# First attention's grouped queries and keys computed channel-first, two heads of different groups in each pair

## The reference

```
proj = jnp.einsum('bsd,df->bsf', h, w_in)
c_q, c_kv, k_r, q_s, k_s, v_s = _split_cols(proj, AB_SPLITS)      # 384, 256, 32, 512, 128, 128
logits = jnp.einsum('bcqkgd,bcskd->bckgqs', qc, kb) * d ** -0.5 + alibi
p = jax.nn.softmax(jnp.concatenate([logits, sink], -1), axis=-1)[..., :-1]
o = jnp.concatenate([o_a.reshape(B, S, -1), o_b.reshape(B, S, -1)], -1)
return jnp.einsum('bsf,fd->bsd', o, w_out)
```

## Time and profile before

| | |
|---|---|
| time, three runs | 923.5 us median (923.07 to 923.65) |
| profiled execution | 923.53 us, span 921.4 us, granted clock 0.999 |
| PE, PEld | 907.3 us (98%), 760.9 us (83%) |
| DVE, ACT, POOL | 607.7 us (66%), 507.5 us (55%), 37.0 us (4%) |
| DMA | 72,556 packets, 169.39 MB, mean 184 GB/s |
| DMA packets under 512 B | 11,304 |

### The profile page before, as it was taken

One profiled execution on the slowest core, in us unless ns is written; L12 is line 12 of the kernel. 1 busy time (PEld: TensorE's weight loads), 2 busy tenths in 40 slices (PEclk: granted clock), 3 DMA queues, 4 the chain that ended last, 5 costly groups with the idle time before them and its releaser, 6 DMA issues.

```text
span 921.4 us, 12745 instructions
## 1 busy us (share of the span) xinstructions
PE 907.3 (98%) x4734; PEld 760.9 (83%) x4734; DVE 607.7 (66%) x999; ACT 507.5 (55%) x816; POOL 37.0 (4%) x53
## 2 busy tenths in 40 slices
PE   7999999999999999999999999999999999999997
PEld 5888878888888898877888888877888888888875
DVE  4888687766663767768766666376656577574665
ACT  4785564655552456666455555255457664655434
POOL 1100034000000001000000000001000000000000
PEclk9999999999999999999999999999999999999999
DMA  8754456755574578443855557354663465545651
GB/s 312 258 183 137 141 191 200 269 190 189 190 237 137 129 202 249 132 162 142 282 170 188 195 191 242 124 180 145 194 202 132 157 203 163 167 155 182 204 170 60
DMA packets 72556, 169.39 MB, mean 184 GB/s; under 512 B 11304, under 2 KB 33216, under 8 KB 71856
## 3 DMA queue, kind: packets, MB, share of 16 engines
q1 hardware_dynamic: 69680, 156.10, 51.3%
q0 software_dynamic: 2816, 12.48, 4.3%
HBM read 167.49 MB, written 1.06 MB: 183 GB/s over the span
## 4 chain that ended last, share of the span: by engine, by line
PE 93%; DVE 3%; ACT 2%; DMA 2%; issue 0%; SPq 0%; DVEq 0%; ACTq 0%
PE psum L733 19%; PE psum L901 14%; PE psum L682 8%; PE psum L684 8%; PE psum L687 8%; PE psum L905 7%; PE psum L934 7%; PE psum L939 3%; PE psum L825 3%; PE psum L835 3%; PE psum L829 3%; PE psum L1036 2%; PE psum L1067 1%; PE psum L654 1%; PE psum L1050 1%; DVE base_lo L1579 1%
## 5 line engine op out<-in xcount | busy, mean ns | idle before, releaser
L1579 DVE TENSOR_TENSOR base_lo<-stage,base_hi 128x1024 fp32r<-128x1024 f32 (+3 forms) x222 | 262.6, 1206 | 98.0 <-ACT base_hi L1206 96.9
L1206 ACT CAST base_hi<-stage 128x1024 fp32r<-128x1024 f32 (+3 forms) x222 | 223.8, 1035 | 53.6 <-PE psum L687 25.7
L1579 DVE TENSOR_TENSOR extra_lo<-stage,extra_hi 128x1024 fp32r<-128x1024 f32 (+1 forms) x68 | 80.0, 1202 | 47.9 <-ACT extra_hi L1206 47.5
L682 PE MATMUL psum<-base_hi,xt 128*128 128x512 f32 (+2 forms) x272 | 107.7, 396 | 0.6 <-ACT xt L1241 0.3
L684 PE MATMUL psum<-base_lo,xt 128*128 128x512 f32 (+2 forms) x272 | 105.3, 387 | 0.4 <-DVE base_lo L1579 0.4
L687 PE MATMUL psum<-base_hi,xt 128*128 128x512 f32 (+2 forms) x272 | 105.1, 386 | 0.0
L1206 ACT CAST extra_hi<-stage 128x1024 fp32r<-128x1024 f32 (+1 forms) x68 | 68.2, 1031 | 49.7 <-PE psum L733 33.0
L901 PE MATMUL psum<-xt,extra_hi 128*128 128x512 f32 x320 | 87.3, 394 | 0.0
L733 PE MATMUL psum<-base_hi,ht 128*128 128x512 f32 x288 | 87.3, 393 | 0.0
L934 PE MATMUL psum<-xt,base_hi 128*128 128x512 f32 x240 | 76.5, 403 | 0.0
L901 PE MATMUL psum<-xt,base_hi 128*128 128x512 f32 x256 | 69.8, 394 | 0.0
(11 more groups left out here) (230 smaller groups left out, 1536.0 us busy)
## 6 DMA issues: line engine op xcount, KB each, us to landing
stage<-in_w_up SPq DMA_DIRECT2D x80, 512.0 KB, 4.4
stage<-in_w_down SPq DMA_DIRECT2D x44, 512.0 KB, 4.5
stage<-in_w_in_a SPq DMA_DIRECT2D x22, 512.0 KB, 4.8
stage<-in_w_cd_in SPq DMA_DIRECT2D x16, 512.0 KB, 4.8
stage<-in_w_in_b SPq DMA_DIRECT2D x12, 512.0 KB, 3.6
stage<-in_w_ab_in SPq DMA_DIRECT2D x11, 480.0 KB, 6.0
ln_par<-in_ln POOLq DMA_DIRECT2D x4, 1024.0 KB, 7.6
stage<-in_w_ab_out SPq DMA_DIRECT2D x8, 512.0 KB, 3.5
```

Of the source, the lines that this page charges most:

```text
L682: pe.matmul(acc, ah, wh, start=(k == 0), stop=False)
L1206: act.copy(w_hi(c, 0, w), stage_of(c, w)).then_inc(hi_done, 1)
L1579: dve.tensor_tensor(w_lo(c, 0, w), stage_of(c, w), w_hi(c, 0, w).bitcast(F32), ALU.subtract).then_inc(lo_done, 1)
```

## The change

The projection's columns are dealt to three products, over the same 5.9 MB of weights:

- `ab_in` stays token-first but keeps only 800 columns (the compressed ones, the rotary key, and the two value heads) in 2 steps of 400, still 2 slices of k in a chunk: chunks 0 to 7.
- `ab_qk`, channel-first, 2 steps of 256 columns, 4 slices in a chunk: chunks 8 to 11. Its blocks of 128 columns are the two key heads, and three pairs of query heads.
- `ab_q`, channel-first, 1 step of 128 columns, 8 slices in one chunk: chunk 12. It is the last pair of query heads.

Pair p is now heads p and p + 4, one of either group, in the halves of a block, so that the block of the two keys serves all pairs as it lies. `turn_pair`, `copy_pair` and `copy_key` go for pairs 0 to 3; the logits read `swa_t`, five blocks of 256 columns in the part of the arena that `proj0` no longer takes. The first pair's logits wait for the last turn of the compressed keys and values instead, since these turns now use banks 6 and 7. The matrix lies in HBM by whole rows of 1,440 columns, and a chunk is gathered in pieces: one of 400 columns (step 0 of `ab_in`), one of 272 and two of 64 (step 1), four of 64 (`ab_qk`), two of 64 (`ab_q`). The first four chunks of `ab_out` are loaded in two DMAs of 64 partitions, since the heads' order differs. The memory's norm moves from chunk 4 to 5, its second half's transposes, `cq`'s and `ckv`'s stay at the same chunk numbers (8, 9, 10), and the split of the chunks due at 7 is put ahead of the low-rank norms. The first pair's logits move from after chunk 11 to after chunk 12.

```diff
-    table = [("ab_in", 8, 2, 480, 3), ("uq", 3, 3, 256, 3), ...
+    table = [("ab_in", 8, 2, AB_TOKEN // 2, 2), ("ab_qk", 8, 4, 256, 2),
+             ("ab_q", 8, 8, 128, 1), ("uq", 3, 3, 256, 3), ...
+TOKEN_COLUMNS = [(0, SWA_AT, "ab_in", 0)] + [(SWA_AT + HD * e, HD, "ab_in", SWA_AT + SWA_GROUP * e + HD)
+                                             for e in range(SWA_KV)]
+SWA_BLOCKS = [(2 * HD * b + HD * e, HD, "ab_in", SWA_AT + SWA_GROUP * e + (HD * (b + 1) if b else 0))
+              for b in range(1 + SWA_H // SWA_KV) for e in range(SWA_KV)]
...
-        TURN_BANKS = {"cq": (2, 3), "ckv": (2, 3)}
+        TURN_BANKS = {"cq": (6, 7), "ckv": (6, 7)}
...
-        twice_k = row_g[:, 0:TT * SWA_KV * 2 * HD].rearrange("p (t g n) -> p t g n", t=TT, g=SWA_KV)
+        swa_t = arena[:, PROJ0 + TT * AB_TOKEN:Q0].rearrange("p (b n) -> p b n", n=S)
...
+                if g.name == "ab_out" and n < SWA_H // 2:
+                    for e in range(2):
+                        sp.dma_start(stage_of(c, WIDTH[c])[e * HD:(e + 1) * HD, :],
+                                     d["w_ab_out"][2 * e + n // 2][n % 2 * HD:(n % 2 + 1) * HD, :]
+                                     ).then_inc(staged[STAGE[c]], 16)
...
             def multiply_pair(p):
-                if p < 8:
-                    pe.wait_ge(pair_copied, p + 1)
+                if p == 0:
+                    pe.wait_ge(turn_lo, turned_at("ckv", 1, 1))
+                if p < 4:
+                    pe.wait_ge(*(read("ab_q", 1) if p == 3 else read("ab_qk", 1 + (p > 0))))
+                elif p < 8:
+                    pe.wait_ge(pair_copied, p - 3)
...
+                        if p < 4:
+                            q, k = swa_t[rows, 1 + p, :], swa_t[rows, 0, :]
...
             # PE's program
             gemm("ab_in", xt_hi, xt_lo, 0, "x0",
-                 {7: lambda: turn("mem", tile_of(mem_x), [(rms_done, 1)], [0]),
-                  8: lambda: turn("mem", tile_of(mem_x), [(rms_done, 2)], [1]), 
-                  9: turn_queries,
-                  10: lambda: [heads_banks("cq"), attend("ab_in", 10),
-                               turn("ckv", tile_of(proj0, Q_RANK), [(rms_done, 6)])],
-                  **attending("ab_in", 11)},
+                 {7: lambda: turn("mem", tile_of(mem_x), [(rms_done, 1)], [0])},
                  second=lambda t: turn("x0", tile_of(x), [(loaded[f"x{t}"], 16)], [t]))
+            blocks("ab_qk", xt, {0: lambda: turn("mem", tile_of(mem_x), [(rms_done, 2)], [1]),
+                                 1: turn_queries, 2: lambda: turn("ckv", tile_of(proj0, Q_RANK), [(rms_done, 6)])})
+            blocks("ab_q", xt, attending("ab_q", 0))
...
             # ScalarE's program
+            def first_queries():
+                copy_block_lows("ab_qk", 0)
+                turn("cq", ht_hi, 8)
+                act.preload_act_table(ACT.Exp)
+            def first_pair():
+                copy_block_lows("ab_q", 0)
                 act.wait_ge(loaded["heads"], 16)
-                attend("ab_in", 10)
+                attend("ab_q", 0)
-                 {4: memory_norm, 7: lambda: [turn("mem", ht_hi, 0, [0]), low_rank_norms()],
+                 {5: memory_norm, 7: lambda: [turn("mem", ht_hi, 0, [0]), split_to(done["due"]), low_rank_norms()]})
+            gemm("ab_qk", None, {0: lambda: turn("mem", ht_hi, 0, [1]), 1: first_queries,
+                                 2: lambda: turn("ckv", ht_hi, 11),
+                                 3: lambda: [copy_block_lows("ab_qk", 1), attend("ab_qk", 3)]})
+            gemm("ab_q", None, {0: first_pair})
...
             # VectorE's program
             def copy_pair(p):
-                dve.wait_ge(pair_turned, p + 1)
-                if p:
+                dve.wait_ge(pair_turned, p - 3)
+                if p > 4:
                     dve.wait_ge(pair_logits, p)
-                if p >= 4:
...
-                else:
-                    last = dve.tensor_copy(qk_t[:, p % 2, :], psum[:, QK_BANK, :])
...
-            def copy_key(g):
...
+            gemm("ab_qk", None, {0: lambda: turn("mem", ht_hi, ht_lo, 0, [1]),
+                                 1: lambda: [add_block_lows("ab_qk", 0), turn("cq", ht_hi, ht_lo, 8)],
+                                 2: lambda: turn("ckv", ht_hi, ht_lo, 11),
+                                 3: lambda: [add_block_lows("ab_qk", 1), attend("ab_qk", 3)]})
```

More of the change, by code:

```diff
@@ L64, in plan_gemms @@
 def plan_gemms():
-    table = [("ab_in", 8, 2, 480, 3), ("uq", 3, 3, 256, 3), ("ukv", 2, 2, 512, 2), ("mem_k", 8, 4, 256, 2),
+    table = [("ab_in", 8, 2, AB_TOKEN // 2, 2), ("ab_qk", 8, 4, 256, 2),
+             ("ab_q", 8, 8, 128, 1), ("uq", 3, 3, 256, 3), ("ukv", 2, 2, 512, 2), ("mem_k", 8, 4, 256, 2),
              ("mem_v", 8, 2, 512, 1), ("ab_out", 8, 1, 1024, 1), ("up0", 8, 2, 512, 11), ("down0", 22, 1, 1024, 1),
@@ L176, in pieces_of @@
         return [(0, g.n, "cd_in", pair_block(j, 0))]
+    if g.name == "ab_in":
+        return runs(TOKEN_COLUMNS, j * g.n, (j + 1) * g.n)
+    if g.name in ("ab_qk", "ab_q"):
+        lo = 2 * HD * (SWA_H // SWA_KV) if g.name == "ab_q" else j * g.n
+        return runs(SWA_BLOCKS, lo, lo + g.n)
     if g.name == "in_ga":
@@ L185, in loads_of @@
 def loads_of(g, n):
+    if g.name == "ab_out" and n < SWA_H // 2:
+        return 2
     return max(1, len(pieces_of(g, n)))
@@ L218 @@
 STREAMS = {"moba": (0, 6), "xa": (6, 10)}
-L0_PLACES = ([("ab_in", 10), ("ab_in", 11)] + [("uq", n) for n in range(3)] + [("ukv", n) for n in range(2)]
+L0_PLACES = ([("ab_qk", 3), ("ab_q", 0)] + [("uq", n) for n in range(3)] + [("ukv", n) for n in range(2)]
              + [("mem_k", n) for n in range(4)] + [("mem_v", n) for n in range(4)] + [("ab_out", n) for n in range(4)])
@@ L454, in block_sums @@
             u = PRODUCTS[name].u0 + j
-            both = psum[:, 2 * (u % 2):2 * (u % 2) + 2, :]
+            count = PRODUCTS[name].n // P
+            both = psum[:, 2 * (u % 2):2 * (u % 2) + count, :]
             if name == "in_c" and j >= 2:
@@ L459, in block_sums @@
                 at = 2 * j
-            return base + j + 1, u, dst[:, at:at + 2, :], both[:, :, 0:S], both[:, :, S:2 * S]
+            return base + j + 1, u, dst[:, at:at + count, :], both[:, :, 0:S], both[:, :, S:2 * S]
         def gates_made(h):
@@ L468, in to_turn @@
             hd = head_of(h)
-            if 8 <= h < 16 or h >= 32:
-                return [hd.q(0), hd.q(1), hd.k(0), hd.k(1)]
-            both = lambda m: view(m, 0, [[1, 2 * HD]])
-            keys = [twice_k[:, t, h // 4, :] if h < 8 else both(hd.k(t)) for t in range(TT)]
-            return [both(hd.q(t)) for t in range(TT)] + keys
+            return [hd.q(0), hd.q(1), hd.k(0), hd.k(1)]
         def keys0(hd):
@@ L542, in _ @@
                             cut = slice(m * FIRST, (m + 1) * FIRST)
-                            sp.dma_start(stage_of(0, WIDTH[0])[:, cut], d["w_ab_in"][0][:, cut]).then_inc(landed, 16)
+                            sp.dma_start(stage_of(0, WIDTH[0])[:, cut].rearrange("p (k n) -> p k n", k=1),
+                                         columns("ab_in", m, 1, 0, FIRST)
+                                         ).then_inc(landed, 16)
                     if g.c0 + n == NS - 1:
@@ L923, in blocks @@
                     pe.wait_ge(acc_free[u % 2], 2 * (u // 2))
-                    for m in range(2):
-                        n = 2 * j + m
+                    cps = g.kc // g.kp
+                    for m in range(cps):
+                        n = cps * j + m
                         c = g.c0 + n
@@ L929, in blocks @@
                             for high in ((True, False) if k < g.kc - 1 else (False, True)):
-                                for b in range(2):
+                                for b in range(g.n // P):
                                     acc, at = psum[:, 2 * (u % 2) + b, :], kk * g.n + b * P
@@ L998, in turn_pair @@
             def turn_pair(p):
-                if p < 2:
-                    pe.wait_ge(*read("ab_in", 2 + p))
-                if p < 4:
-                    pe.wait_ge(key_twice, p // 2 + 1)
                 if p == 4:
@@ L1060, in sum_pair @@
                     pe.wait_ge(o_lo, p)
-                if 4 < issued["turned"] <= 8:
+                if issued["turned"]:
                     pe.wait_ge(pair_copied, issued["turned"])
```

86 lines of the change are left out of this document (38 added, 48 removed).

## The result

The kernel after takes 927.86 us (median of 8 runs), the kernel before 924.08 in the same session: a ratio of 1.0041 [1.0031, 1.0051], 3.8 us slower. The profiled execution took 927.61 us. The forecast was 925.8, slower, in a range of 920.6 to 931, its own 923.8 to 928.5.

A forecast was written before the change was run, and what follows sets the result against it. The prediction took PE, busy 98% of the span, as the bound: 923.53 - 2.4 (PE's sum) + 4.7 (stall for late weights) = 925.8 us. Range 920.6 to 931, the forecast's own 923.8 to 928.5.

The forecast's parts named there:

- The stall: PE ahead of the memory's second turn: chunk 9 lands late behind the mask load, ScalarE's in-order work follows, +4.7 us.
- the course without a wait: PE past the memory's second turn at 33.2 us if no weights came late, against 37.9 with the stall.
- The packet's price: DMA engine time per packet of the new weight loads, by straight lines between profile rows: 20.8 ns at 256 B.
- Rival B: Weight loads: a 256 B packet costs what 512 B does, 31 ns; chunk 9 3.9 us later, 929.7 us; chance 0.13.
- PE's sum: PE's own work, waits and start together: 0.2 - 1.6 - 0.8 - 0.2 = -2.4 us.
- The transposes' -1.6: Pairs 0 to 3 each lose four transposes on PE: 0.47 + 0.43 + 0.35 + 0.35, -1.6 us.
- The waits' -0.8: PE's waits for VectorE's doubled key (0.5 us) and a pair's statistics (0.3 us) both go, -0.8 us.
- The 0.3: PE's wait for a pair's statistics, taken as gone because VectorE is a copy and a key copy lighter between masks.
- The products' +0.2: PE's projection products: same streamed columns, 32 matmuls more, at most 0.2 us, taken as +0.2.
- the start's -0.2: First pass, paced by arrivals: fewer columns per matmul give back -0.2 us, between 0 and -0.5.
- Rival A: Loads stay hidden, chunk 9 lands before about 29 us, only PE's sum is left: 921.1 us; chance 0.27.
- C: Middle case: chunk 8 or 9 gets through before the masks, stall 1 to 3 us, within 0.2% of 923.5; chance 0.24.

The follow-up runs named there:

- experiment 3: Kernel after with 14 spare matmuls of 512 columns filling PE's wait ahead of the memory's second turn: 927.23 us, 1.0033 of the kernel before.
- experiment 1: Kernel after with weights of ab_in, ab_qk and ab_q packed chunk by chunk, one DMA each: 924.24 us, 0.9994 of the kernel before.
- experiment 8: Kernel after with only the HBM column order changed, each chunk one piece, packets of 1,600, 1,024 and 512 B: 924.33 us, 1.0003 of the kernel before.
- experiment 2: Kernel after with GpSimd asking for the masks three chunks later, small packets kept: 923.25 us, 0.9986 of the kernel before.
- experiment 9: Kernel before with chunks 4 to 7 loaded in three pieces and 8 to 11 in eight: 930.54 us, 1.0077 of the kernel before.
- experiment 7: Kernel after with late masks and 16 spare transposes at the old places of pairs 0 to 3: 923.66 us, 0.9993 of the kernel before.
- experiment 6: Kernel after with late masks and VectorE making pair 0's and 1's masks before a chunk's low part: 922.43 us, 0.9979 of the kernel before.
- experiment 5: Kernel after with both packed weights and late masks: 922.31 us, 0.9981 of the kernel before.
- experiment 4: Kernel after with chunk 9's split put behind step 1's evacuation and the memory copies: 927.73 us, 1.0033 of the kernel before.

## Why the prediction was right, and where its sizes were off

*The stall: mechanism right, composed wrongly.* I had chunk 7 at 24, the mask load at 25.5 and chunk 9 at 33.9 us. The trace has the mask load at 24.73 and chunk 9 at 32.9. PE was to be past the second turn at 37.9; it is at 37.70. The gap to the course without a wait, +4.7, compares with 5.0, but it came as 3.27 us of idle time and 1.7 of work at the low clock. I had added up the engines' chain and left out PE's clock. That 4.7 and 5.0 lie so near each other is partly luck: chunk 9 came 1.0 us earlier than forecast, and the clock, which the sum left out, put 1.7 on top. By experiment 3 the time would have been only some 0.6 us shorter without the clock's fall. I also counted the new DMAs by their packets alone and put SyncE's time to ask for them at nothing, without a reason; it is mostly 0.5 us or more for each, and chunk 9 was asked for 2 us later than in experiment 1. Experiments 1 and 8 take the small pieces away, experiment 2 the masks in front, and each ends the stall; 9 makes a stall in the kernel before, with even more DMAs; 3 shows the clock.

*The packet's price.* 20.8 ns for 256 B was no value between two rows but the line drawn on below 315 B (and 54.6 ns at 1,088 B should have been 54.1, which changes nothing). 18.3 was measured by wall time, which says when a chunk lands. By the busy share, as the prediction had counted its rows, it is 18.3 x 1.348 = 24.6 ns, because packets overlap. Rival B's floor (31 ns) is refuted by either. The Trainium skill (DMA: Bandwidth & Descriptors, Specifications) puts a limit at 512 B, below which writes become read-modify-write; the trace shows lower throughput, 218 GB/s against 393, but no extra price of a packet, which by wall time is cheaper than the line through the rows said.

*PE's sum: -2.4 predicted, about -0.9 found by the spans,* and -0.7 to -1.3 by experiment 2 against the kernel before. Two steps failed. The transposes' -1.6 took each group at its whole distance on PE. Experiment 7 puts them at 0.4 to 0.6 in the time, give or take 0.8. Behind pair 0's logits PE is bound to the chain on VectorE and ScalarE (experiment 6), and a transpose less there only lengthens a wait. The waits' -0.8: the 0.5 for the key did go, with its cause. The 0.3 became 0.75, for the same reason, and a wait of 0.6 us for a copy of the probabilities (line 1089) came up a little later. The copies that I counted as relief for VectorE had lain in VectorE's own wait for the exponentials. The products' +0.2 and the start's -0.2 are too small to be seen beside a start that scatters by 2 us.

*The sum.* -0.9 + 5.0 gives the +4.1 of the spans; -2.4 + 4.7 gave +2.3. The time was inside the forecast's own range, 2 us over its centre. Rival A is what experiment 2 gives, at 923.25 and not 921.1, because the PE sum was too good. C did not occur.

*What stays open.* Whether it is the size of the packets or the number of DMAs that makes chunk 9 late enough: every run that changed one changed the other, and four DMAs with large packets, or one with small ones, were not tried. Where nothing held SyncE up, it asked for a chunk of `ab_qk` in 2.2 us (experiment 2, from 26.58 to 28.78 us), and the engines moved one in 2048 x 18.3 / 16 = 2.3 us, so the two are close. Whether small packets cost anything beside the masks (the 0.5 to 0.9 us between experiments 2 and 5), and `ab_out`'s eight DMAs, which weren't tried alone; they are asked for from 83.9 to 96.5 us, and the offset to the kernel before does not grow there (4.3 us at 60 us, 3.9 at 115), so they can't be much.

## What to carry to other kernels

When an edit changes how weights lie in HBM, price its packets and count its DMAs, and then ask what else is asked for when these land: here the small pieces cost less than 1 us alone and the early masks some 1 us, and both together cost 5. One late chunk in front of an engine that works in order is paid by all that stands behind it, and moving the chunk in that order only moved the wait. Work that is taken off PE counts only where PE sets the pace: look at which chain ends at the next wait before you add it up.

## What the runs showed of the hardware

- *A queue starved.* With GpSimd's queue moving large packets, SyncE's queue with packets of 256 B got 17 packets to 33, 1.9% of the engines to 96.6%, in 1 us; in experiment 9 it got 3. The Trainium skill (DMA: Bandwidth & Descriptors, Queues, rings and completion order) says that each engine takes turns between its queues. Many rows agree, in the packets that the profile counts: 29 to 29 in after (27 to 28 us, 256 B beside 12 KB), 33 to 33 in experiment 8 (1 KB beside 12 KB), 82 to 81 in experiment 2 (36 to 39 us, 3 KB beside 12 KB). In others q1 has far fewer than its turns: 0 to 37 in after from 28 to 29 us, 2 to 113 in the kernel before. Why is open.
- *PE's clock.* An idle time of 3.27 us (3.0 of it empty in the windows) was followed by a granted clock of 0.50, and the slow work cost 1.6 to 1.7 us; with the same time filled it stayed at 1.00. It fell to 0.50 behind 4.11 us of idle time in experiment 9 too, and behind 2.25 us in experiment 4.
- *VectorE beside GpSimd.* Two operations on 128 x 2 elements took 0.99 us (experiment 1) and 0.97 (experiment 7) while GpSimd's affine select ran (0.86 us), and 0.36 without it. The Trainium skill (SBUF — State Buffer, Terms) has one port pair that the two engines hold exclusively; the rows agree.
- *Small packets alone.* 5,257 of them in 6 us, 18.3 ns each over 16 engines.
- *Asking for a DMA.* SyncE's timeline has 0.33 us for a chunk in one piece of 3,200 to 4,096 B a packet (experiment 1), 0.37 to 2.4 for each of the pieces of 512 packets of 256 B in after, and 0.70 on average for the 32 in experiment 9.
